# A two-layer decoder trunk on one core: next layer's parameters loaded in the perceptron, compressed softmax two tasks ahead, four weight units split on another engine

## What is computed

```
for l in range(DEPTH):                                   # 2 layers
    proj = einsum('btd,dn->btn', x, w_in[l])             # 1024 -> 2578
    (qa, ka, va, u, qc, kcm, vcm, ksl, vsl, kwi, vwi, gc) = split(proj)
    o_a = diff_attention(rope(qa), rope(ka), va, lam)    # 6 heads, two softmaxes each
    o_b = pool_mixer(u, w_pool[l], pool_scale[l])        # means over 2/4/8/16 rows
    # o_c: 6 heads, compressed + selected + window branches, mixed by sigmoid gates
    p_cmp = where(cmask, softmax(where(cmask, q @ kc * scale, -1e30)), 0)   # 31 compressed keys
    mix = concat(o_a, o_b, o_c) @ w_out[l]
    x = layer_norm(ALPHA * x + mix, ln1_g[l], ln1_b[l])
    x = layer_norm(ALPHA * x + square(relu(x @ w_up[l])) @ w_down[l], ln2_g[l], ln2_b[l])
```

## Time and profile before

| | us |
|---|---|
| median of 3 runs | 1309.37 (1308.35 to 1309.49) |
| the profiled execution | 1308.09 |
| its span | 1306.1 |
| PE busy in it | 1258.2 (96%) |
| DVE, POOL, ACT busy | 727.1 (56%), 512.1 (39%), 478.9 (37%) |

### The profile page before, as it was taken

How to read it: one execution, slowest core, us unless ns; L and a number is a source line. 1 busy time by engine, 2 the same in 40 slices (tenths; PEclk the granted TensorE clock), 3 DMA queues, 4 the chain that set the end, 5 groups by cost and what they waited for, 6 DMA issues and landing times.

```text
span 1306.1 us, 17938 instructions
## 1 busy us (share of the span) xinstructions
PE 1258.2 (96%) x7154; PEld 1038.3 (79%) x7154; DVE 727.1 (56%) x1125; ACT 478.9 (37%) x958; POOL 512.1 (39%) x290
## 2 busy tenths in 40 slices
PE   7999988999999999999989999899999999999996
PEld 7998755689888888888889976557898888888885
DVE  4394588439763262350476756874596723614506
ACT  5325576724322222221233355766233222212210
POOL 3465121044444444444334732111445444444443
PEclk9999999999999999999999999999999999999998
DMA  7423001042333333333153220011334333333311
GB/s 248 119 77 95 2 1 38 29 129 79 132 97 97 97 97 97 97 97 93 36 129 103 84 66 1 18 33 47 99 98 137 98 99 95 98 96 95 98 56 65
DMA packets 68834, 110.10 MB, mean 84 GB/s; under 512 B 15056, under 2 KB 27664, under 8 KB 68624
## 3 DMA queue, kind: packets, MB, share of 16 engines
q1 hardware_dynamic: 67600, 104.77, 26.6%
q10 hardware_dynamic: 1152, 4.19, 0.9%
HBM read 106.85 MB, written 2.10 MB: 83 GB/s over the span
## 4 chain that ended last, share of the span: by engine, by line
PE 89%; DVE 6%; ACT 1%; SPq 1%; DMA 1%; issue 1%; DVEq 0%; POOL 0%; ACTq 0%
PE ps L647 17%; PE ps L648 16%; PE ps L649 16%; PE ps L644 9%; PE ps L643 9%; PE ps L645 9%; PE ps L704 4%; PE ps L716 3%; PE ps L752 2%; DVE probs L1346 1%; DVE negmax L1298 1%; PE ps L602 1%; PE ps L737 1%; SPq L470 1%; DVE probs_a L1346 1%; PE ps L827 1%
## 5 line engine op out<-in xcount | busy, mean ns | idle before, releaser
L507 POOL TENSOR_TENSOR w_lo<-raw,w_hi 128x1024 fp32r<-128x1024 f32 (+3 forms) x192 | 439.8, 2295 | 648.8 <-ACT w_hi L934 648.3
L934 ACT ACTIVATE w_hi<-raw 128x1024 fp32r<-128x1024 f32 (+3 forms) x200 | 198.5, 993 | 609.7 <-PE ps L649 371.5
L643 PE MATMUL ps<-xt_hi,w_lo 128*128 128x512 f32 (+1 forms) x576 | 210.7, 366 | 0.0
L644 PE MATMUL ps<-xt_hi,w_hi 128*128 128x512 f32 (+1 forms) x576 | 210.5, 365 | 0.0
L645 PE MATMUL ps<-xt_lo,w_hi 128*128 128x512 f32 (+1 forms) x576 | 210.5, 365 | 0.0
L647 PE MATMUL ps<-w_hi,xt_lo 128*128 128x384 f32 (+3 forms) x448 | 151.9, 339 | 7.7 <-ACT pe_t L999 4.6
L647 PE MATMUL ps<-w_hi,mt_lo 128*128 128x512 f32 x384 | 150.1, 391 | 0.0
L648 PE MATMUL ps<-w_hi,mt_hi 128*128 128x512 f32 x384 | 149.5, 389 | 0.0
L649 PE MATMUL ps<-w_lo,mt_hi 128*128 128x512 f32 x384 | 149.4, 389 | 0.0
L649 PE MATMUL ps<-w_lo,xt_hi 128*128 128x384 f32 (+3 forms) x448 | 148.5, 331 | 0.0
L648 PE MATMUL ps<-w_hi,xt_hi 128*128 128x384 f32 (+3 forms) x448 | 148.4, 331 | 0.0
(11 more groups left out here) (168 smaller groups left out, 1905.0 us busy)
## 6 DMA issues: line engine op xcount, KB each, us to landing
raw<-in_w_up SPq DMA_DIRECT2D x64, 512.0 KB, 3.7
raw<-in_w_down SPq DMA_DIRECT2D x64, 512.0 KB, 3.8
raw<-in_w_in SPq DMA_DIRECT2D x32, 384.0 KB, 3.6
raw<-in_w_in SPq DMA_DIRECT2D x8, 512.0 KB, 4.0
raw<-in_w_out SPq DMA_DIRECT2D x8, 512.0 KB, 3.3
raw<-in_w_out SPq DMA_DIRECT2D x12, 256.0 KB, 3.8
raw<-in_w_in SPq DMA_DIRECT2D x8, 274.0 KB, 2.9
xres<-in_x SPq DMA_DIRECT2D x4, 512.0 KB, 6.1
```

The lines of the kernel that those rows point to most:

```text
L507: nc.gpsimd.tensor_tensor(unit_of(w_lo, u), unit_of(raw, u), unit_of(w_hi, u).bitcast(F32), ALU.subtract).then_inc(s_lo_ready, 1)
L643: mm(o, wl[:, c], a_hi[:, k, cols], start=first, stop=False)
L644: mm(o, wh[:, c], a_hi[:, k, cols], start=False, stop=False)
L934: A(unit_of(w_hi, u), unit_of(raw, u), ACT.Copy).then_inc(s_hi_ready, 1)
```

## The change

1. The parameters of layer 1 are loaded inside the perceptron of layer 0, four before each of the units U_MLP+12 to U_MLP+16, behind a wait for the first layer norm of layer 0. The wait at L448 is gone, and units 4 to 11 of layer 1 follow units 0 to 3 directly.
2. The compressed scores change places with the pool mixer's `box` in SIDE (steps 6 and 8), and every later step of the compressed softmax comes two tasks sooner: maximum in 8, exp in 10, sum and reciprocal in 11; the factor stays in 13. The scores now lie in a part of `proj_b`. The mask of 0 and 1 for each element is replaced by one value for each row, multiplied into the reciprocal (24 values a partition) on DVE; POOL's full product with the mask is gone.
3. The remainders of the units U_OUT to U_OUT+3 are computed by DVE in steps 21, 27, 29 and 31; ACT rounds them in 20, 26, 28 and 30.
4. DVE's copies of turned tiles 2 and 3 move ahead of the last row tile of the `qc` rotation.
5. ACT copies the seventh chunk's row tile before, not behind, the SIDE work of its step. The first `square_sums` evacuation (step 11) moves from DVE to ACT, with its constant as a bias.

```diff
+PARAMS = 20
+OUT_SPLIT = (20, 26, 28, 30)
-SIDE = {2: (("compress", 0, 5), ("turn", 9, 6)), 4: (("turn", 10, 5), ("turn", 11, 6)), 6: (("box", 0, 5), ("box", 1, 6)),
-        8: (("cmp_scores", 0, 5), ("cmp_scores", 1, 6)), 10: (("square_sums", 0, 5),),
+SIDE = {2: (("compress", 0, 5), ("turn", 9, 6)), 4: (("turn", 10, 5), ("turn", 11, 6)), 6: (("cmp_scores", 0, 5), ("cmp_scores", 1, 6)),
+        8: (("box", 0, 5), ("box", 1, 6)), 10: (("square_sums", 0, 5),),
...
-    k[:, K_CM:K_CB] = seen.reshape(P, -1)
+    k[:, K_CM:K_CB] = seen[:, :, 0]
...
-        cmp_s = at("cmp_s", rc + 12288, [TT * 6, 32])
+        cmp_s = proj_b[:, :, T_QC - T_VCM:T_QC - T_VCM + 192].rearrange("p i (s n) -> p i s n", n=32)
...
-                if layer:
-                    sp.wait_ge(s_x_normed, nth("x_normed", layer - 1, 2 * TT))
-                else:
+                if layer == 0:
                     sp.dma_start(kc[:, P:K_END], consts[:, P:K_END]).then_inc(s_const_in, 16)
                     sp.dma_start(rows[:, 0, 0:P], consts[:, K_MASK:K_MASK + P]).then_inc(s_const_in, 16)
                     sp.wait_ge(s_blk_zero, 1)
+                    parameters(0, 0, PARAMS)
...
+                    if layer < DEPTH - 1 and U_MLP + 12 <= u < U_MLP + 17:
+                        sp.wait_ge(s_x_normed, nth("x_normed", layer, TT))
+                        parameters(layer + 1, 4 * (u - U_MLP - 12), 4 * (u - U_MLP - 11))
                     unit(layer, u)
...
-                for tt in range(3):
-                    rope_k(tt)
+                rope_k(0)
+                rope_k(1)
                 pool.wait_ge(s_cmp_max, nth("cmp_max", layer, 1))
-                nc.gpsimd.tensor_tensor(cmp_s[:], cmp_s[:], over24(0), ALU.subtract).then_inc(s_cmp_shifted, 1)
+                nc.gpsimd.tensor_tensor(cmp_s, cmp_s, over24(0), ALU.subtract).then_inc(s_cmp_shifted, 1)
+                rope_k(2)
                 rope_k(3)
                 pool.wait_ge(s_cmp_factor, nth("cmp_factor", layer, 1))
-                link(nc.gpsimd.tensor_tensor(cv, cv, cm, ALU.mult))
-                nc.gpsimd.tensor_tensor(cmp_s[:], cmp_s[:], over24(3), ALU.mult).then_inc(s_cmp_probs, 1)
-                split(layer, U_OUT, U_MLP + 2)
+                nc.gpsimd.tensor_tensor(cmp_s, cmp_s, over24(3), ALU.mult).then_inc(s_cmp_probs, 1)
+                split(layer, U_OUT + 4, U_MLP + 2)
...
+                    elif kind == "square_sums":
+                        last = A(rms[:, c], b, ACT.Identity, scale=1.0 / DV, bias=lams[:, 7:8])
...
-                    if t in (20, 24, 28, 32):
-                        split_to(layer, U_OUT + t // 4 - 4)
-                    if t == 12:
+                    if t in OUT_SPLIT:
+                        split_to(layer, U_OUT + OUT_SPLIT.index(t) + 1)
+                    if t == 10:
                         act.wait_ge(s_cmp_shifted, nth("cmp_shifted", layer, 1))
...
-                    if t - 1 in SIDE:
-                        side(t - 1)
                     if t < 3 * TT and t % 3 == 2:
...
                         copy_in(layer, LAST, t // 3)
+                    if t - 1 in SIDE:
+                        side(t - 1)
...
                 for tt in range(TT):
+                    if tt == TT - 1:
+                        copy_early(2)
+                        copy_early(3)
                     rotate(V.tensor_tensor, link, tt, ((T_QC, 6, 64, R_CCQ, R_SCQ),)).then_inc(s_roped_c, 1)
...
-                    if t == 10:
-                        dve.wait_ge(s_side_emptied, nth("side_emptied", layer, SIDE_END[8]))
+                    if t == 8:
+                        dve.wait_ge(s_side_emptied, nth("side_emptied", layer, SIDE_END[6]))
...
+                    if t == 11:
+                        dve.wait_ge(s_cmp_exp, nth("cmp_exp", layer, 1))
+                        by_slot = cst[:].rearrange("p a (i s) -> p a i s", i=TT)
+                        link(V.tensor_reduce(by_slot[:, 1], cmp_s, AX.X, ALU.add))
+                        link(V.reciprocal(cst[:, 2, :], cst[:, 1, :]))
+                        link(V.tensor_tensor(by_slot[:, 2], by_slot[:, 2],
+                                             kc[:, K_CM:K_CM + TT].unsqueeze(2).to_broadcast([P, TT, 6]), ALU.mult))
...
+                    if t - 1 in OUT_SPLIT:
+                        low_unit(layer, U_OUT + OUT_SPLIT.index(t - 1))
```

More of the change, by code:

```diff
@@ L438, in unit, with parameters @@
                             .then_inc(s_raw[u % RING], 16)
[L440 to L445, removed]
-                if layer:
-                    sp.wait_ge(s_x_normed, nth("x_normed", layer - 1, 2 * TT))
-                else:
-                    sp.dma_start(kc[:, P:K_END], consts[:, P:K_END]).then_inc(s_const_in, 16)
-                    sp.dma_start(rows[:, 0, 0:P], consts[:, K_MASK:K_MASK + P]).then_inc(s_const_in, 16)
-                    sp.wait_ge(s_blk_zero, 1)
+            def parameters(layer, first, end):
                 loads = []
@@ L467, in _ @@
                 loads.append((cmp_wv[:, :, 0, :], w_cmp_k[layer].rearrange("(j h) d e -> (h d) j e", h=2)))
-                assert 16 * len(loads) == PER_LAYER["params"]
-                for dst, src in loads:
+                assert len(loads) == PARAMS
+                for dst, src in loads[first:end]:
                     sp.dma_start(dst, src, allow_slow_non_contiguous=True).then_inc(s_params, 16)
+            for layer in range(DEPTH):
+                for u in range(RING):
+                    unit(layer, u)
+                    if layer == 0 and u % 2 == 0:
+                        for tt in (u, u + 1):
+                            sp.dma_start(xres[:, tt], x[0, tt * P:(tt + 1) * P, :]).then_inc(s_x_in[tt], 16)
+                if layer == 0:
+                    sp.dma_start(kc[:, P:K_END], consts[:, P:K_END]).then_inc(s_const_in, 16)
+                    sp.dma_start(rows[:, 0, 0:P], consts[:, K_MASK:K_MASK + P]).then_inc(s_const_in, 16)
+                    sp.wait_ge(s_blk_zero, 1)
+                    parameters(0, 0, PARAMS)
                 for u in range(RING, UNITS):
@@ L1014, in side @@
                     for n, (kind, c, bank) in enumerate(SIDE[t]):
-                        if kind in ("turn", "box", "compress", "cmp_turn"):
+                        if kind in ("turn", "box", "compress", "cmp_turn") or (kind == "square_sums" and c == 0):
                             act.wait_ge(s_side_ready, nth("side_ready", layer, SIDE_FIRST[t] + n + 1))
@@ L1292, in _ @@
                     V.tensor_copy(qa[q][:] if q < Q_KA else ka[:, q - Q_KA, :], ps[:, bank, :]).then_inc(s_turned_dve, 1)
+                for tt in range(TT):
+                    if tt == TT - 1:
+                        copy_early(2)
+                        copy_early(3)
+                    rotate(V.tensor_tensor, link, tt, ((T_QC, 6, 64, R_CCQ, R_SCQ),)).then_inc(s_roped_c, 1)
+                    dve.wait_ge(s_roped_c, nth("roped_c", layer, tt + 1))
+                dve.wait_ge(s_lam_exp, nth("lam_exp", layer, 1))
+                link(V.tensor_tensor(lams[:, 4:5], lams[:, 3:4], lams[:, 2:3], ALU.subtract))
+                link(V.tensor_tensor(lams[:, 5:6], lams[:, 4:5], kc[:, K_LAM + 2 * layer:K_LAM + 2 * layer + 1], ALU.subtract))
+                copy_early(4)
+                copy_early(6)
                 def negative_max(t):
@@ L1370, in _ @@
                     if t == 13:
-                        dve.wait_ge(s_cmp_exp, nth("cmp_exp", layer, 1))
-                        link(V.tensor_reduce(cst[:, 1, :], cmp_s[:], AX.X, ALU.add))
-                        link(V.reciprocal(cst[:, 2, :], cst[:, 1, :]))
                         gv = gates[:].rearrange("p i (g j r) -> p i j g r", g=2, r=3)[:, :, :, :, 0]
```

32 lines of the change are left out of this document (12 added, 20 removed).

## The result

The changed kernel took 1289.88 us in the median of four runs (1287.21, 1287.22, 1292.53, 1294.10) against 1309.43 for the kernel before: ratio 0.9851, interval [0.9814, 0.9887]. Five later runs gave 1287.36, 1287.42, 1292.41, 1292.97 and 1294.99, ratio 0.9860 [0.9837, 0.9883]. The times lie on two levels. The four near 1287.3 have a mean granted clock of 0.997; the five from 1292.4 up have 0.990 or 0.991. The forecast for the median was 1287.5, with a range of 1284 to 1294. The first median lies between the two levels, where none of the nine runs lies. The profiled run is one of the first kind, 1287.22 with a span of 1285.3, which is to be held against 1308.09 and 1306.1.

A forecast was written before the change was run, and what follows sets the result against it. PE bounds the kernel, busy 1258.2 of 1306.1 us, so only its waits and low-clock stretches can be won: 5.57 + 2.58 + 11.4 + 1.54 = 21.1 us, 1308.09 to 1287.0, median 1287.5; own range 1285 to 1290, with rivals 1284 to 1294.

The forecast's parts named there:

- Seam: Between the layers: PE's 4.22 us wait falls to 0.40, winning 3.82 us, and 1.75 us of half-clock products behind it go.
- Sixth chunk: PE's wait before the sixth chunk goes because DVE's two copies come earlier: 1.29 us a layer, 2.58 in all.
- Before task 8: Attention: ACT's row tile moves into idle time, so PE's 0.98 us wait for task 6's exp shrinks by 0.68 a layer.
- Task 15: Attention: earlier sums and no POOL mask product cut PE's 2.70 us wait for DVE by 2.3 a layer, leaving 0.4.
- Tasks 24 and 28: Attention: with POOL's splits gone there, PE's waits of 1.38 and 1.67 us for DVE shrink by 1.38 and 1.35 a layer.
- The other units on DVE: Steps 21, 29 and 31: DVE is ahead of PE, so cost nothing; bounds 0 and 3.66 us a layer.
- The box and square_sums copies on ACT: They delay the exps of tasks 10 and 12 by about 2 and 1.6 us, within their room: no cost, bounds 0 and 3.6 a layer.
- Clock in layer 1's tasks: Tasks 28 to 34 of layer 1: the stretch at 1.2 GHz behind the 1.67 us stand goes, winning 1.54 us.
- Rivals 3, 4 and 5: 3: weight ring late, 9.87 us, 0.04; 4: seam wait stays, 5.57 us, 0.03; 5: splitting stalls DVE, 1319.4 us, 0.03.
- Rival 1: Attention waits find another releaser, ACT: gains before task 8 and at task 15, 5.96 us, fail; 1293.5 us, chance 0.17.
- Rival 2: The clock falls elsewhere: both stretches at 1.2 GHz, 3.3 us, return at other stands; 1290.8 us, chance 0.15.

## Why the prediction came out

The forecast was 1287.0 on the scale of the profiled run and 1287.5 for the median; the profiled run took 1287.22, the medians 1289.88 and 1292.41. By its steps:

- *Seam, 3.82 + 1.75.* The wait won 3.79; the slow products 1.54 (3.85 less the 2.31 that the same stretch won in layer 0). Shown by doing it alone (5.4 us between like starts) and undoing it (5.2). One reading was off: the clock had not fallen during the stand. It was still 1.00 until 674.25 and 0.50 from 674.50, 0.3 us after PE went on at 674.18; at 872.15 it was the same.
- *Sixth chunk, 1.29.* 1.53 a layer by undoing; the bracket of a wait that goes wholly is too small a price. *Before task 8, 0.68.* 0.73.
- *Task 15, 2.3.* 2.50: 1.39 from the sums, 0.84 from POOL's product; the wait of 0.4 that was to remain did not. POOL's product still held DVE's two weights by 0.44 us (1.19 against 0.75), not by the 0.9 forecast. The total was near, its second part a quarter less than said.
- *Tasks 24 and 28, 1.38 + 1.35 = 2.73.* 3.36 from the turn at 185.23 on. Task 28 kept 0.16 instead of 0.3, and a wait of 0.33 us between them, which I had not priced, went too: with the units on POOL it is there again (at 198.74). The three brackets give 1.38 + 0.33 + 1.51 = 3.22, the other 0.14 fits the overlap seen at the sixth chunk, which is argued and not shown here.
- *The other units on DVE, nothing.* The wait at task 34 stayed at 0.91, so nothing.
- *The box and square_sums copies on ACT, nothing, "the second just so".* This step failed by a little: -0.36 a layer. The exps of task 12 stood behind the copy, as the waits of 0.29 and 1.06 and the kernel with the sums in step 10 show.
- *Clock in layer 1's tasks, 1.54.* 4.90 - 3.36 = 1.54.

The parts gave 1.4 us more than forecast, and the start and end of that run took 1.7 back; that the total was met to 0.2 us is luck to that extent. It is luck too that the profiled run was one of the four of nine that kept their clock.

Rivals 3, 4 and 5 are refuted by runs. Rival 1 is true to 0.36 us a layer. Rival 2, that the clock falls elsewhere, got 0.15 and 3.3 us. It is what decides the median: five of nine runs fell, and they lie 5 to 8 us over the others, so that the medians are 1289.9 and 1292.4, where 1287.5 was forecast. The later median lies outside the 1285 to 1290 that the forecast gave itself without its rivals. What failed was to read the clock out of one profile: that the profiled run of before kept its clock at the waits of 167 to 181 us said nothing on other runs, and the kernel with only the parameters moved, whose waits there are the same, had a stretch at 1.2 GHz in layer 0. The profiled run's 0.995 was itself rare: 21 of the 23 runs of the kernel before that were taken beside the experiments have 0.987 to 0.993. The price was low as well: a stretch costs 1.4 to 6.0 us here, not 1.5.

Open is what makes the clock fall. It fell more often the longer the waits around steps 12 and 13 were in sum: in 1 of 4 passes (one layer of one profile) with 1.40 us, in 8 of 16 with 1.72, in 4 of 4 with 2.56 or 3.00 (`square_sums` back on DVE, ACT's old order). But these are few passes, and length alone does not decide: in the kernel before and the one with the parameters moved, waits of 1.51 us in sum with one of 2.70 us behind them were followed by a fall in 1 of 4. Waits of 1.37 and 1.67 alone, at tasks 24 and 28, were followed by none in four passes (the two kernels with units on POOL), but the same ones by one each in the kernel before and in the one with the parameters moved. By whole runs, 7 of 8 with the shorter waits kept 0.997, 4 of 9 of the changed kernel; that is suggestive, not settled.

## What to carry to other kernels

Ask of each wait who would be the next releaser, and price it by the like place in another layer where the disturbance is absent; that gave the seam's wait to 0.03 us. Measure what a wait costs from a start before it to a start behind it: where products overlap, its bracket is too small, here 1.29 for 1.53 us. When work moves to an engine in order, what counts is what it waits for and who stands behind it: with the same copy on DVE, PE waited 1.57 us in one order and 0.52 in another. Take several profiles, or the mean clock of several runs, before a median is explained, since small waits close together can cost many times their length.

## What the runs showed of the hardware

- A stretch at 1.2 GHz cost 1.4 to 6.0 us, three waits of 1.72 us in sum; the same kernel with the same waits has it in some runs and not in others. Behind the kernel before's stands of 4.22 and 1.67 us the clock fell 0.3 us after PE had gone on, not during the stand.
- Two DVE instructions over 384 columns took 1.19 us when they began 0.8 us into a POOL product of 1.48 us, and 2.42 us when a second POOL product followed it; the second weight ended 0.2 us after POOL. With POOL idle two such take 0.75 us. A DVE product over 2 elements took 2.11 us instead of 0.16 under a POOL split.
- 20 small loads ahead of four weight loads of 512 KB moved PE by less than 0.1 us over 405 us.
